# Cached pages of a paged attention stored with their transpose, in rows of 288 words

## The reference

```python
# per sample b: 16 pages of 128 keys, found through page_table; 4 heads x 4 tokens = 16 query rows
s = einsum('bthc,bsc->bhts', q_lat, ckv) + einsum('bthr,bsr->bhts', q_pe, kpe)   # ckv: 128 words a key, kpe: 32 words a key
probs = softmax(scale * concat([s_pages, s_own]))
out = einsum('bhts,bsc->bthc', probs, ckv)
```

## Time and profile before

| | |
|---|---|
| median of 3 runs | 1837.69 us (1837.42 to 1839.45) |
| the profiled execution | 1840.06 us, of which the span from first to last instruction is 1838.2 us |
| PE busy | 1757.1 us, 96% of the span |
| stage of the samples, layer 1 | 121.93 to 219.94 us |
| stage of the samples, layer 2 | 1032.75 to 1128.18 us |
| read from memory | 245.80 MB |

### The profile page before, as it was taken

The page is one execution under the profiler, slowest core; times in us unless marked ns, Lnnn a source line. Parts: engine busy times, 40 slices in busy tenths (PEclk is TensorE's granted clock), DMA queues, the critical chain, the costliest instruction groups (busy, mean ns, idle before and its releaser), DMA issues.

```text
span 1838.2 us, 27159 instructions
## 1 busy us (share of the span) xinstructions
PE 1757.1 (96%) x10832; PEld 1302.1 (71%) x10832; DVE 576.3 (31%) x1320; ACT 451.2 (25%) x979; POOL 113.1 (6%) x190
## 2 busy tenths in 40 slices
PE   7999899999999999999999989999999999999997
PEld 5676567777767767777766755676777677777775
DVE  1431266332022253330034324652320240633201
ACT  3233233132031231110132342321311332311101
POOL 1003000010010010000010030000100100100000
PEclk9999999999999999999999999999999999999999
DMA  8522322165337433343164133221733473333431
GB/s 309 155 97 82 137 77 85 67 235 192 115 137 292 171 120 138 137 142 114 65 244 160 29 88 149 83 82 47 292 133 139 150 307 122 113 136 137 142 114 49
DMA packets 66767, 256.75 MB, mean 140 GB/s; under 512 B 8529, under 2 KB 36626, under 8 KB 39378
## 3 DMA queue, kind: packets, MB, share of 16 engines
q1 hardware_dynamic: 54722, 199.52, 30.8%
q0 software_dynamic: 11360, 54.21, 7.9%
q10 hardware_dynamic: 560, 1.30, 0.2%
HBM read 245.80 MB, written 9.19 MB: 139 GB/s over the span
## 4 chain that ended last, share of the span: by engine, by line
PE 89%; DVE 5%; ACT 2%; issue 2%; DMA 1%; ACTq 0%; POOL 0%; DVEq 0%; POOLq 0%
PE banks L789 41%; PE banks L818 16%; PE banks L740 6%; PE banks L773 6%; PE banks L796 5%; PE banks L847 4%; PE banks L737 4%; PE banks L745 3%; PE banks L1048 1%; DVE work L1912 1%; PE banks L1017 1%; PE banks L1439 1%; ACT work L1523 1%; PE banks L1458 1%; DMA weight_ring<-in_w 1%
## 5 line engine op out<-in xcount | busy, mean ns | idle before, releaser
L789 PE MATMUL banks<-h_normed,weight_ring 128*128 128x288 f32 x1888 | 459.4, 406 | 1.1 <-ACT h_normed L1523 1.1
L789 PEld LDWEIGHTS banks<-h_normed,weight_ring 128*128 128x128 f32 x1888 | 358.6, 190 | 100.5 <-ACT h_normed L1523 1.5
L818 PE MATMUL banks<-h_normed,weight_ring 128*128 128x288 f32 x1024 | 280.9, 418 | 4.6 <-ACT values_by_token L1695 4.6
L818 PEld LDWEIGHTS banks<-h_normed,weight_ring 128*128 128x128 f32 x1024 | 189.2, 191 | 64.6 <-issue 8.5
L789 PE MATMUL banks<-work,weight_ring 128*128 128x288 f32 (+1 forms) x960 | 226.8, 399 | 1.8 <-issue 1.8
L789 PEld LDWEIGHTS banks<-work,weight_ring 128*128 128x128 f32 x960 | 182.2, 190 | 46.1 <-issue 2.6
L1523 ACT ACTIVATE work<-banks 128x512 f32<-128x512 f32 (+7 forms) x206 | 94.2, 457 | 283.2 <-PE banks L745 74.2
L1912 DVE TENSOR_TENSOR squares<-squares 128x288 f32<-128x288 f32 (+2 forms) x40 | 20.3, 508 | 329.4 <-ACT squares L1561 329.2
L773 PE MATMUL banks<-h_normed,weight_ring 128*128 128x288 f32 x448 | 116.3, 411 | 0.0
L773 PEld LDWEIGHTS banks<-h_normed,weight_ring 128*128 128x128 f32 x448 | 83.1, 191 | 28.6 <-issue 8.1
L847 PE MATMUL banks<-h_normed,weight_ring 128*128 128x288 f32 x288 | 81.7, 445 | 19.8 <-DMA weight_ring<-in_w 13.6
(11 more groups left out here) (302 smaller groups left out, 1703.2 us busy)
## 6 DMA issues: line engine op xcount, KB each, us to landing
weight_ring<-in_w SPq DMA_DIRECT2D x171, 1024.0 KB, 4.8
work<-in_mem_k POOLq DMA_DIRECT2D x12, 1024.0 KB, 11.0
work<-in_mem_v POOLq DMA_DIRECT2D x12, 1024.0 KB, 9.4
work<-in_pool SPq DMA_DIRECT2D x128, 80.0 KB, 2.1
weight_ring<-in_pool SPq DMA_DIRECT2D x64, 80.0 KB, 2.0
projected<-in_mem_k POOLq DMA_DIRECT2D x4, 1024.0 KB, 24.9
projected<-in_mem_v POOLq DMA_DIRECT2D x4, 1024.0 KB, 6.2
weight_ring<-in_pool POOLq DMA_DIRECT2D x32, 80.0 KB, 2.2
```

Source lines behind the costliest of these rows:

```text
L789: last = mm(ps[:, bank, 0:width], block_of(first + k), rhs(k), start=k == 0, stop=k == n - 1)
L818: last = mm(ps[:, BANK[g], 0:N], block_of(t[2] + k), H[:, k, :] if t[0] == "gate" else O[:, 2 * n + k, :], start=k == 0, stop=k == t[3] - 1)
```

## The change

The host stores each page as 128 rows of 288 words: 128 latent words of key p; 128 words of the transposed latent block (latent word p of all 128 keys); and 32 words of the rotary part, turned in quarters (word p % 32 of the 32 keys of quarter p // 32). A page is one transfer of 144 KB. `turns`, `pack_rotated` and ACT's 40 copies a layer are gone; `scores(b)` reads the page as it lies, the latent part in four products as before, the rotary part in 16 products of 128 columns in place of one of 512.

Where the pages lie, and which slots wait for which sample:

```diff
-        kv_after = {4: SLOT * (N_IN - 3), 5: SLOT * (N_IN - 1), 6: SLOT * (N_IN - 1) + KD}
-        slot_after = {N_IN: 4, N_IN + 1: 4, N_IN + 2: 5, N_IN + 3: 6, N_IN + 4: 6}
...
+        whole = groups(work, 0, 11)
+        lent, o_half, first = groups(slots, 3 * SLOT * P, 3), groups(of, 4 * N, 1), groups(slots, 0, 4)
+        kv = [whole[0:4], whole[4:8], lent + o_half, whole[8:11] + first[:1],
+              whole[0:4], whole[4:8], whole[8:11] + o_half, first]
...
+        slot_after = {N_IN: 3, N_IN + 1: 3, N_IN + 2: 7}
```

A sample's pages lie in four parts of four pages (page p in part p % 4), and `cache` can load some parts alone. SP:

```diff
-                        for b in {4: [0], 6: [1], 8: [2, 3]}.get(s, []):
-                            cache(sp, layer, b)
-                    for b in (4, 6):
-                        sp.wait_ge(*at("gemm_done", block_done(kv_after[b])))
-                        cache(sp, layer, b)
+                        for b, parts in {4: [(0, range(4))], 7: [(1, range(4))], 10: [(2, (3,))]}.get(s, []):
+                            cache(sp, layer, b, parts)
+                    sp.wait_ge(*at("gemm_done", slot_done(N_IN - 4)))
+                    cache(sp, layer, 2, (0, 1, 2))
+                    sp.wait_ge(*at("mla_pv", 1))
+                    cache(sp, layer, 4)
                     for s in range(N_IN, NSLOT):
                         if s in slot_after:
                             sp.wait_ge(*at("mla_pv", slot_after[s] + 1))
                         slot(s)
+                        if s == N_IN + 1:
+                            sp.wait_ge(*at("mla_pv", 4))
+                            cache(sp, layer, 6)
```

POOL, behind the store of the rotated keys:

```diff
-                    pool.wait_ge(*at("gemm_done", block_done(kv_after[5])))
+                    cache(pool, layer, 3, (0,))
+                    pool.wait_ge(*at("mla_ol", 2))
+                    cache(pool, layer, 3, (1, 2))
+                    pool.wait_ge(*at("gemm_done", slot_done(N_IN - 3)))
+                    cache(pool, layer, 3, (3,))
+                    pool.wait_ge(*at("mla_pv", 2))
                     cache(pool, layer, 5)
-                    pool.wait_ge(*at("mla_pv", 1))
+                    pool.wait_ge(*at("gemm_done", slot_done(N_IN - 1)))
+                    pool.wait_ge(*at("mla_pv", 4))
                     cache(pool, layer, 7)
```

PE's `scores`:

```diff
                         g, f = b // 2, b % 2
-                        pe.wait_ge(*at("pages_copied", 5 * b + 5))
-                        mm(ps[:, g % 2, :], m_qpz[:, g, P * f:P * f + P], m_krt, start=f == 0, stop=True, skip_group_check=True)
+                        bank = S_BANK[g]
+                        if b == 4:
+                            pe.wait_ge(*at("mla_olc", 2))
+                        pe.wait_ge(*at(f"kv_full{b}", 16 * PAGES))
+                        out = [ps[32 * j:32 * j + 32, bank, :].rearrange("p (i k) -> p i k", i=4) for j in range(4)]
                         for j in range(4):
-                            last = add(ps[32 * j:32 * j + 32, g % 2, :], m_qz[:, g, 32 * f:32 * f + 32], m_kt[:, j, :])
+                            mm(out[j], m_qz[:, g, 32 * f:32 * f + 32], turned(b, j), start=f == 0, stop=True, skip_group_check=True)
+                        for k in range(0, P, 32):
+                            for j in range(4):
+                                last = add(out[j][:, :, k:k + 32], m_qpz[:, g, P * f + k:P * f + k + 32], rotary(b, j))
                         last.then_inc(S("page_scores"), 1)
```

More of the change, by code:

```diff
@@ L247 @@
         (6, "rw_tok rw_tokc"),
-        (8, "ca_o_s ca_ss_s mixed mla_pv page_scores rotated_packed"),
+        (8, "ca_o_s ca_ss_s mixed mla_pv page_scores"),
         (12, "rows_free"),
@@ L403, in program @@
         m_po = sqf[:, 1152:1152 + NS]
[L404 to L412, removed]
+        m_selr = sqf[:, 1184:1216]
+        m_sums = sqf[:, 1216:1218]
+        m_recs = sqf[:, 1218:1219]
+        m_tops = sqf[0:1, 1220:1220 + NS]
+        m_row = sqf[0:1, 1252:1252 + P]
+        m_pot = sqf[0:NS, 1380:1380 + P]
+        m_os = sqf[:, 1508:1764]
         prf = PR[:, :, :].rearrange("p a b -> p (a b)")
@@ L1080, in _ @@
[L1080 to L1090 removed]
+                    scores(0)
+                    scores(1)
+                    fill(4)
+                    maxima(0)
+                    scores(2)
+                    maxima_back(0)
+                    scores(3)
@@ new lines, in _ @@
+                    shares(0)
+                    fill(4)
+                    values(0)
+                    fill(4)
+                    outputs(0)
+                    fill(2)
+                    maxima(1)
+                    fill(2)
+                    maxima_back(1)
+                    fill(3)
+                    shares(1)
+                    fill(4)
+                    values(1)
+                    fill(4)
+                    outputs(1)
+                    fill(2)
+                    scores(4)
@@ new lines, in _ @@
+                    fill(3)
+                    scores(5)
+                    mix(3)
+                    maxima(2)
+                    mix(5)
+                    maxima_back(2)
+                    scores(6)
+                    shares(2)
+                    mix(7)
+                    values(2)
+                    scores(7)
+                    outputs(2)
+                    mix(8)
+                    maxima(3)
+                    mix(9)
+                    maxima_back(3)
+                    mix(12)
@@ L1091, in _ @@
+                    shares(3)
+                    mix(13)
+                    values(3)
+                    mix(15)
+                    outputs(3)
+                    mix(16)
                     pe.wait_ge(*at("mla_ols", NB // 2))
@@ L1629, in _ @@
                         late_out()
+                    wait("ml_abs")
+                    step(A(l_t[0:4, :], l_t[0:4, :], ACT.Exp))
+                    step(A(l_t[0:4, :], l_t[0:4, :], ACT.Ln, bias=one[0:4, :]), "ml_log")
                     wait("mla_ql")
```

172 lines of the change are left out of this document (51 added, 121 removed).

## The result

The changed kernel takes 1845.15 us (median of 5 runs, 1842.06 to 1846.09), the kernel before 1837.42 beside it (5 runs): a ratio of 1.0046, interval 1.0033 to 1.0059. It is 7.7 us slower, where 1833.1 was forecast; the range ended at 1843. The kernel before, run again beside each series of experiments, took 1835.57 to 1837.42 us; a difference of some 2 us between the times of two series says nothing, and each ratio is to the kernel before in its own series.

The account below looks back on a forecast made before the run. PE, busy 96% of the span, was taken as the bound. Per layer 25.8 + 2.5 + 39.8 + 3.3 + 20.5 + 2.5 = 94.4 us against 98.0 and 95.4, 4.6 less in all: 1833.1 us, range 1820 to 1843.

Parts of the forecast that it names:

- The start shifts: Ahead of the stage: eight fill blocks move there, 3.9 us, plus a 1.3 us wait for ACT's copy; 5.3 us later.
- T: When mla_pv reaches 1, behind sample 3's first values; predicted at 25.8 us, before the clock charge of 2.5.
- Half clock behind sample 3: PE's clock falling to half at the wait for sample 3's pages; charged 2.5 us, which shifts T.
- The end: From sample 6's scores to uv: 20.5 us, with sample 7's pages there by about T + 48, just in time.
- the mixed window: Earlier profile stretch with pages among slots moving 400 GB/s at full use; spoke for more than 315, so 370 was taken.
- disappears in the one for 6: Clock loss after the shorter wait for sample 4, said to vanish in sample 6's wait; nothing charged.
- The 3.3 us of contention: Pages of samples 4 and 5 sharing the engines: sample 4 2.8 us late, plus 0.5 for overlap of 6 and 7.
- the longest wait: PE's wait before sample 6's scores, predicted as the longest: 9 us, near 12 with contention.
- the work of PE is the same: Ahead of the stage and behind it PE's work was taken as unchanged, so only the time to uv was computed.
- B: Rival: the clock doesn't fall at sample 3, or queues hinder each other less; 1823, or 1819 with light contention; chance 0.24.
- C: Rival: slower; two page streams share the engines at 255 GB/s, sample 4 7.9 us late, all reaching sample 6; 1843.3, chance 0.20.
- D: Rival: pages in time and PE stays the bound, uv at 66 us; 1776, chance 0.04.

Follow-up runs that it names:

- e3_fill: Changed kernel with the last three blocks of the fills done ahead of sample 4's scores, not behind them; 1843.15 us, ratio 1.0031 to the kernel before.
- e4_ml: Changed kernel with SP waiting for the two loads of load_ml before issuing slot N_IN + 3; 1843.27 us, ratio 1.0032 to the kernel before.
- e13_num7: Changed kernel with POOL loading sample 7's 16 page numbers right behind sample 5's issues, before waiting for the last fill; 1843.75 us, ratio 1.0050.
- e9_slot: e6_num_all plus the moves of e4_ml and e14_slot_late; 1791.15 us, ratio 0.9757 to the kernel before.
- e14_slot_late: Changed kernel with slot N_IN + 1 issued behind sample 6's pages instead of behind sample 4's; 1847.24 us, ratio 1.0053 to the kernel before.
- e11_num3: Changed kernel with POOL loading the last 12 page numbers of sample 3 before its wait for mla_ol; 1831.95 us, ratio 0.9981 to the kernel before.
- e5_num_sp: Changed kernel with SP loading the 32 page numbers of samples 4 and 6 before its wait for mla_pv; 1821.54 us, ratio 0.9915.
- e6_num_all: e5_num_sp with POOL too loading the numbers of samples 3, 5 and 7 before the waits guarding their pages; 1807.95 us, ratio 0.9828.

## Why the prediction was wrong, step by step

**Right.** The start shifts by 4.5 us with a wait of 1.15 for ACT's copy (5.3 and 1.3 predicted). The scores cost 1.06 and 1.06 us. T came 23.4 us behind the own keys' start, 23.0 predicted: sample 3's wait was 5.5 instead of 3.8, the rest came sooner. Half clock behind sample 3, charged 2.5, cost about 2.3: 4.6 us of work at half speed.

**The step that failed** is in "The end": sample 7's pages "are there by about T + 48, just in time". They came at T + 52.0, and PE was there at T + 47.8. Two things moved them. Sample 4 landed at T + 24.8 instead of T + 23: the sum took 370 GB/s for two page streams, and while both queues issued the engines moved 318, near the 315 that the prediction had worked out from the earlier trace rows and then set aside for the mixed window. At 318 its own working gives 4.7 us of delay for sample 4 in place of 2.8; 4.5 were measured (T + 24.8, against the T + 20.3 that it gave for sample 4 alone). And behind that wait its scores and the last fill ran at half clock, 6.3 us instead of 3.6. POOL's loads and issues hang on that fill, so both delays, 4.5 us together (1.8 and 2.7), went into sample 7. PE, on the other side, was there 2.3 us earlier than in the sum. The half clock behind sample 4 had been charged at nothing, since it "disappears in the one for 6": for PE it does; for POOL, which waits for PE's fill, it doesn't.

**Mis-sized.** The 3.3 us of contention were put before sample 6. SP doesn't wait for sample 4's landing before it goes on, so sample 6 came at T + 39.5, its bare chain (39.8), and its wait was 3.7 us, not near 12; the contention fell on sample 4 and through the fill on 7. From sample 6 to `uv` the sum had 23.0 us with the clock, the trace 29.6: the 4.2 of wait, and a tail of 17.1 us from sample 7's scores where e3_fill takes 14.3 at full clock. With -3.6 from T to sample 6, 0.4 at T and -0.8 at the start, `uv` came 2.7 us later than predicted in layer 1, and 2.2 in layer 2. That is 4.9 of the 8.7 us between the sum (4.6 us less) and the traces (4.1 more); the other 3.8 arose behind `uv`. Of the 7.7 us of the medians, 3.8 are in no trace. Of the prediction's signs, the longest wait stood before sample 4, not 6.

**Left out.** The sum counted nothing behind the stage, as "the work of PE is the same" there. Layer 1 lost 2.6 us there. The text named the place (the slots after sample 7's values) but not who queues behind them, `load_ml`, nor the clock. Which of the two it was stays open: DVE's wait for `load_ml` stands in layer 2 too, where nothing was lost, and e4_ml without it gains nothing over both layers (86.4 us for 85.7); the clock was 0.80 for 0.92. The last 1.6 us in layer 2 are not shown to come from the change: 0.6 are a longer wait for `in_mem_v` and 1.5 a half clock over 129 products from 1532 us (32.7 for 31.2), with 0.5 less elsewhere, and in ten of the fourteen experiments the stretch from L1195 to the last instruction is as long as before to within 0.7 us.

**The rivals.** B asked for a clock that doesn't fall at sample 3, or for less contention; the clock was 0.53 from 139 to 146 us, and the contention was heavier than assumed. C gave 1843.3, near the truth, and for that it had luck: it was right that 370 GB/s was too much, but the two page streams moved 318, above C's 255 and above the 310 below which it was to decide; sample 4 came 4.5 us late, not 7.9, and the lateness reached sample 7, not 6. By the rule of the Trainium skill ("DMA: Bandwidth & Descriptors", "Issuing engines are not separate DMA queues") two issuers share the engines; e3_fill and e13_num7 agree, with sample 6's wait at 9.8 and 9.0 us once sample 7 is issued beside it. D, at 1776 with a chance of 0.04, asked for numbers loaded much faster; loaded earlier, and with e9_slot's two small moves, they brought 1791.

## What to carry to other kernels

When the work that hid a transfer is taken away, price the whole chain from the semaphore to the landing: here 9.4 us of register loads, 8.4 to 9.4 of issues, 2.6 to 4.1 of landing for 16 pages, of which the first part needs no permission and can stand ahead of the wait. Follow every delay through the engine that waits for it to whoever waits for that engine, to the last consumer, where nothing hides it any more. And where several chains are late one behind the other, taking away one behind the first tells little (e3_fill, e13_num7 and e14_slot_late each moved the time by some 2 us or less, where the first one, in e11_num3, gave 12 to 13); take all away once for the floor, then add them back.

## What had not been expected of the hardware

Pages with rows of 1152 bytes, issued by SP alone in the changed kernel, and the end of two streams of SP and POOL in e3_fill, with no slot among them:

```profile
124.00:128.00 4.00, 4.00 (x49) 3.39 (x47) 0.00 (x0) 2.40 (x6) 0.00 (x0) 1.00 0.84 238
```

```profile
188.00:192.00 4.00, 0.00 (x0) 0.00 (x0) 0.00 (x0) 0.30 (x2) 1.92 (x4) 0.63 1.05 393
```

While both queues issue, the second one adds a third to the rate: 318 GB/s in the row of 160.64 to 167.65 us, for 238, though the first one's share was 0.84. Scaled to a share of 1.0 the first row would give 283 GB/s, so a share of busy time does not tell what is left. The 393 GB/s are reached only as the issues run out (at 190 us); why the rate rises then, no run shows. With the engines full an issue can take longer; from SP's queue in e5_num_sp:

```profile
171.86 5.38 SPq L601 DMA_DIRECT2D work<-in_pool  x3
```

These three pages of sample 6 took SP 5.38 us at a share of 1.02, against 1.36 in the changed kernel. It need not: in e6_num_all, at a share of 1.05, three took between 1.36 and 2.07.
